# Spreading the inverse RMS norm over the partitions: a row in DRAM, written and read back, in place of two transposes

## The reference

```python
def rms_norm(x, g):
    y = x * rsqrt(mean(x * x, axis=-1) + EPS)
    return y * g

def swiglu(x, w_gate, w_up, w_down):
    return (silu(x @ w_gate) * (x @ w_up)) @ w_down

for l in range(2):
    x = x + 0.5 * swiglu(rms_norm(x, ffn1_norm[l]), ffn1_w_gate[l], ffn1_w_up[l], ffn1_w_down[l])
    ...                                    # the mixing sub-layer
    x = x + 0.5 * swiglu(rms_norm(x, ffn2_norm[l]), ffn2_w_gate[l], ffn2_w_up[l], ffn2_w_down[l])
```

## Time and profile before

| | us |
|---|---|
| median of three executions | 1039.33 |
| the profiled execution | 1040.34 |
| its span, first to last instruction | 1038.5 |
| PE busy | 1032.4 (99%) |
| PEld busy | 891.7 (86%) |
| DVE busy | 718.3 (69%) |
| ACT busy | 586.1 (56%) |
| POOL busy | 61.8 (6%) |
| HBM read | 185.98 MB |

### The profile page before, as it was taken

The page is one execution under the profiler, slowest core; times in us unless marked ns, Lnnn a source line. Parts: engine busy times, 40 slices in busy tenths (PEclk is TensorE's granted clock), DMA queues, the critical chain, the costliest instruction groups (busy, mean ns, idle before and its releaser), DMA issues.

```text
span 1038.5 us, 15559 instructions
## 1 busy us (share of the span) xinstructions
PE 1032.4 (99%) x5648; PEld 891.7 (86%) x5648; DVE 718.3 (69%) x1132; ACT 586.1 (56%) x935; POOL 61.8 (6%) x71
## 2 busy tenths in 40 slices
PE   8999999999999999999999999999999999999998
PEld 7888888998888888888888888889988888888887
DVE  6766666668786876666687666666688868666665
ACT  6555454466963754554565455455678646454552
POOL 0052000121100000000000000001211000000000
PEclk9999999999999999999999999999999999999999
DMA  7665544455435455655445555534454346545541
GB/s 264 248 225 192 204 162 167 140 183 193 146 123 203 173 187 189 205 189 209 179 147 202 202 192 182 210 136 152 154 203 163 122 163 219 205 163 202 191 173 61
DMA packets 35269, 187.53 MB, mean 181 GB/s; under 512 B 4368, under 2 KB 4384, under 8 KB 20128
## 3 DMA queue, kind: packets, MB, share of 16 engines
q1 hardware_dynamic: 34992, 186.51, 51.0%
q0 software_dynamic: 240, 0.53, 0.2%
HBM read 185.98 MB, written 1.05 MB: 180 GB/s over the span
## 4 chain that ended last, share of the span: by engine, by line
PE 99%; DMA 1%; SPq 0%; DVE 0%; ACT 0%; issue 0%
PE ps L1369 96%; PE ps L1803 1%; PE ps L1393 1%; DMA w_raw<-in_w_ffn 1%; PE ps L1832 1%; PE ps L1868 0%; PE ps L1712 0%; PE ps L1704 0%; PE ps L1414 0%; DVE x_cols L999 0%; ACT w_hi L554 0%; SPq L318 0%; SPq L317 0%
## 5 line engine op out<-in xcount | busy, mean ns | idle before, releaser
L1369 PE MATMUL ps<-hT,w_hi 128*128 128x512 f32 x1408 | 341.3, 391 | 1.9 <-ACT w_hi L554 1.9
L1369 PEld LDWEIGHTS ps<-hT,w_hi 128*128 128x128 f32 x1408 | 258.9, 188 | 52.4 <-ACT w_hi L554 2.1
L884 DVE TENSOR_TENSOR w_lo<-w_raw,w_hi 128x2048 fp32r<-128x2048 f32 x82 | 188.0, 2293 | 87.7 <-ACT w_hi L549 87.7
L1369 PEld LDWEIGHTS ps<-hT,w_lo 128*128 128x128 f32 x1408 | 176.8, 188 | 7.5
L1369 PE MATMUL ps<-hT,w_lo 128*128 128x256 f32 x1408 | 178.3, 279 | 0.0
L1369 PE MATMUL ps<-w_hi,hT 128*128 128x512 f32 (+2 forms) x576 | 174.3, 377 | 0.0
L549 ACT ACTIVATE w_hi<-w_raw 128x2048 fp32r<-128x2048 f32 x85 | 162.0, 1906 | 13.9 <-PE ps L1369 13.2
L1369 PE MATMUL ps<-w_lo,aTh 128*128 128x512 f32 x352 | 137.2, 390 | 0.0
L1369 PE MATMUL ps<-w_hi,aTl 128*128 128x512 f32 x352 | 137.0, 389 | 0.0
L1369 PE MATMUL ps<-w_hi,aTh 128*128 128x512 f32 x352 | 136.8, 390 | 0.0
L578 ACT ACTIVATE S<-ps 128x256 f32<-128x256 f32 x88 | 33.7, 383 | 154.6 <-PE ps L1369 154.6
(11 more groups left out here) (168 smaller groups left out, 952.9 us busy)
## 6 DMA issues: line engine op xcount, KB each, us to landing
w_raw<-in_w_ffn SPq DMA_DIRECT2D x85, 1024.0 KB, 4.9
w_raw<-in_w_ffn SPq DMA_DIRECT2D x90, 512.0 KB, 5.7
w_raw<-in_w_gate SPq DMA_DIRECT2D x16, 1024.0 KB, 5.1
w_raw<-in_w_proj SPq DMA_DIRECT2D x16, 592.0 KB, 4.4
w_raw<-in_w_branch SPq DMA_DIRECT2D x8, 1024.0 KB, 4.8
w_raw<-in_w_out SPq DMA_DIRECT2D x8, 1024.0 KB, 4.8
w_raw<-in_w_uq SPq DMA_DIRECT2D x4, 384.0 KB, 3.0
w_raw<-in_w_ffn SPq DMA_DIRECT2D x4, 256.0 KB, 6.6
```

The lines of the kernel that those rows point to most:

```text
L884: dve.tensor_tensor(wl_gu[b], raw_gu[b], wh_gu[b].bitcast(F32), ALU.subtract).then_inc(lo_gu.sem, 1)
L1369: return pe.matmul(dst, w, m, start=start, stop=stop, skip_group_check=True)
```

## The change

In the last three feed-forward sub-layers (layer 0 second half, layer 1 both halves) PE's two transposes and ACT's copy are gone. SP writes `rs` to a DRAM tensor of one row of 256 values (256 elements of 4 bytes, in the order of the tokens, so that the two values of a partition go to places 128 apart), waits until they have landed, and issues a second DMA that reads the row back into all 128 partitions of `rsB`. SP does this between its loads of the gate and up weights of blocks 2 and 3. DVE waits for the second DMA (`rsb_in`), and in these three sub-layers it now adds up both the gate and the up half of block 0 before that wait. The first sub-layer of the kernel keeps its two transposes and the copy (`spread_rs_first`). Nothing else differs.

```diff
--- before.py
+++ after.py
@@ -202,8 +202,10 @@
         gate4_first = signal("gate4_first", 1)
         uq1_first = signal("uq1_first", 1)
         rs_done = signal("rs_done", 3 * RS_STEPS)
-        rsb_ps = signal("rsb_ps", 2)
-        rsb_done = signal("rsb_done", 2)
+        rsb_ps = signal("rsb_ps", 0)
+        rsb_done = signal("rsb_done", 0)
+        rs_written = signal("rs_written", 16 * 2)
+        rsb_in = signal("rsb_in", 16 * 2)
         z_done = signal("z_done", 2 * FB)
         gate_full = signal("gate_full", KC // 2)
         ht_ps = signal("ht_ps", 3 * KC)
@@ -308,6 +310,12 @@
             bank, half = (X_AT_FIRST if layer + n == 0 else X_AT)[c]
             return ps[:, bank, half * SEQ:(half + 1) * SEQ]
 
+        rs_row = nc.dram_tensor("rs_row", (1, SEQ), F32, kind="Internal").ap()
+
+        def spread_count(layer, w):
+
+            return 16 * (2 * layer + w)
+
         block = ctx.enter_context(nc.Block())
 
 
@@ -368,6 +376,14 @@
                         sp.wait_ge(lo_d.sem, lo_d.at(l - 1, 2 * FB - 2 + b))
                     load_d((2 * l + w) * FB + b, b)
 
+            def spread_rs(l, w):
+
+                sp.wait_ge(rs_done.sem, rs_done.at(l, 2 * w * RS_STEPS))
+                with nc.allow_non_contiguous_dma(reason="256 values, once a sub-layer"):
+                    sp.dma_start(rs_row.rearrange("b (t p) -> p (b t)", p=P), rs[:, :]).then_inc(rs_written.sem, 16)
+                sp.wait_ge(rs_written.sem, spread_count(l, w))
+                sp.dma_start(rsB[:, :], rs_row.to_broadcast([P, SEQ])).then_inc(rsb_in.sem, 16)
+
             def load_ffn_rest(l, w):
                 o0 = (0, FFN2_0)[w]
                 first = 0
@@ -383,6 +399,8 @@
                 for b in range(2):
                     sp.wait_ge(lo_gu.sem, lo_gu.at(l, o0 + 2 * first + b))
                     load_gu(row0 + b, b)
+                    if l + w > 0 and b == 0:
+                        spread_rs(l, w)
                 sp.wait_ge(lo_d.sem, lo_d.at(l, w * FB + 2 * first))
                 load_d(row0, 0)
                 with sp.Fori(first + 1, FB // 2 - 1) as i:
@@ -624,9 +642,9 @@
 
                     act.activation(scrap[:, 0:1], scrap[:, 1:2], func)
 
-                def spread_rs(w):
-
-                    act.wait_ge(rsb_ps.sem, rsb_ps.at(l, w))
+                def spread_rs_first():
+
+                    act.wait_ge(rsb_ps.sem, 1)
                     act.activation(rsB[:, :], ps[:, RS_BANK, 0:SEQ], ACT.Copy).then_inc(rsb_done.sem, 1)
 
                 def ffn(w, split_following):
@@ -640,7 +658,7 @@
                         third_high(0)
                         third_high(1)
                         load_table(ACT.Silu)
-                        spread_rs(0)
+                        spread_rs_first()
                         gate_silu(0, 0, 0)
                         split_d(0, 0, 0)
                         prod_high(0, 0, 0)
@@ -665,7 +683,6 @@
                     else:
                         split_d(n, 0, 0)
                         load_table(ACT.Silu)
-                        spread_rs(w)
                         gate_low(n, 0, 0)
                         up_low(n, 0, 0)
                         gate_silu(n, 0, 0)
@@ -1018,7 +1035,7 @@
                         gate_fold(0, 0, 0)
                         up_fold(0, 0, 0)
                         third_low(0)
-                        dve.wait_ge(rsb_done.sem, rsb_done.at(l, 0))
+                        dve.wait_ge(rsb_done.sem, 1)
                         gate_scaled(0, 0, 0)
                         third_low(1)
                         up_times(0, 0, 0)
@@ -1041,9 +1058,11 @@
                         prod_low(0, 0, 3)
                     else:
                         split_d(n, 0, 0)
-                        dve.wait_ge(rsb_done.sem, rsb_done.at(l, w))
-                        gate_z(n, 0, 0)
-                        up_prod(n, 0, 0)
+                        gate_fold(n, 0, 0)
+                        up_fold(n, 0, 0)
+                        dve.wait_ge(rsb_in.sem, spread_count(l, w))
+                        gate_scaled(n, 0, 0)
+                        up_times(n, 0, 0)
                         prod_low(n, 0, 0)
                         gate_z(n, 0, 1)
                         split_gu(n, 0, 2)
@@ -1407,9 +1426,9 @@
                     pe.wait_ge(x_done.sem, x_done.at(layer, 4 * n + (h + 1) * TT - 1 - 2 * TT))
                     transposed(layer, n, h)
 
-                def spread_rs(w):
-
-                    pe.wait_ge(rs_done.sem, rs_done.at(l, 2 * w * RS_STEPS))
+                def spread_rs_first():
+
+                    pe.wait_ge(rs_done.sem, rs_done.at(0, 0))
                     for t in range(TT):
                         ins = pe.transpose(ps[:, RS_BANK, t * P:(t + 1) * P], rs[:, t:t + 1].to_broadcast([P, P]), ident[:, :])
                     ins.then_inc(rsb_ps.sem, 1)
```

## The result

The changed kernel takes 1073.45 us (median of five runs, 1072.39 to 1074.33) against 1039.37 us of the kernel before on the same chip: a ratio of 1.0325, 95% interval 1.0314 to 1.0337. The prediction was 1038.64 us and its range ended at 1040.8. The profiled execution took 1072.5 us, 1.0 us less than its median, and that of before 1.0 us more than its own; so the span grew by a little less than the median, from 1038.5 to 1070.7 us.

The account below looks back on a forecast made before the run. PE was taken to bound the kernel, so 3 x 0.23 = 0.69 us of transposes came off in full, the DMAs (4.4 us) being hidden: median 1039.33 - 0.69 = 1038.64 us, range 1038.2 to 1040.8.

Parts of the forecast that it names:

- What bounds the kernel, and what the transposes cost: PE sets the pace, with two waits at the very start; two transposes cost it 0.23 us in each of three sub-layers.
- the 0.69 worked out: Us taken off PE's list by removing the transposes: 3 x 0.23 in the three changed sub-layers.
- By when rsB is needed: DVE's multiplication by rsB may start at 348.50, 531.80 and 862.50 us without making PE wait at block 0's down product.
- budgets of 5.40, 4.97 and 5.39: Us from the end of POOL's power to the latest harmless multiplication by rsB, in the three changed sub-layers.
- What the two DMAs take: Write 2.1 us, read back 2.2 us, handovers 0.1 us: 4.4 us in all, hidden from PE.
- high end of 6.4 us: Upper bound for the write, from posq_i, a transfer of 256 4-byte values on POOL's queue in the other direction.
- its 5.2 us: Upper bound for the read back, from a smaller broadcast row (rows, 36 KB) among weight loads.
- the 11.7 us of both: Both DMAs at their upper bounds plus handovers, 6.4 + 5.2 + 0.1: 19.3 us late in all, net +18.6 us (1058).
- Rival C: Slow write of single 4-byte values, 6.4 us: rsB late by 10.3 us, net +9.6, about 1049.0 us; chance 0.10.
- What else moves: DVE's multiplication starts 0.6 us later; SP's load for block 3 goes at about 345.6, not 345.41, covered by 1.6 us.
- The range: Execution 1038.2 to 1040.8 us, upwards to 5.95 us from POOL's power to the multiplication, leaving out the slow write, 0.10.

Follow-up runs that it names:

- e4: The changed kernel without its two DMAs and DVE's wait for them, three sub-layers reusing the first one's rsB: 1038.55 us against 1039.39 before.
- probe1: The kernel before plus single DMAs behind its last store, each waited for: 256 x 4 B landed in 8.2 and 8.4 us side by side, 1.5 us 512 B apart.
- probe2: The kernel before plus single DMAs behind its last store, with other pitches and rows: 1 KB written as one run landed in 1.1 us.
- e5: The changed kernel with the 256 values written 64 B apart and the row's first 1024 B read back, so not the norm: 1040.48 us.
- e8: The kernel before, with its transposes, plus the write of rs to DRAM, read by nobody and not waited for until the program's end: 1052.14 us.
- e1: The kernel before, with its transposes, plus the write of rs to DRAM, which SP waits for and nobody reads: 1056.79 us.
- e3: The changed kernel with both DMAs and the wait between them issued from GpSimd's queue in place of SP's: 1081.27 us, one run.
- e2: The changed kernel with each partition's two values written side by side (128 pieces of 8 B) and rsB read at a stride of two: 1050.31 us.
- e9: The changed kernel writing 8 B every 16 B into a 2 KB row, multiplying by every second pair, block 3's load held until rsB landed: 1041.07 us.

## Why the prediction was wrong, point by point

- **What bounds the kernel, and what the transposes cost:** right. PE's eight high matmuls take 1.85 us without them. e4 gained 0.84 us for the 0.69 worked out; its interval reaches none, but its trace shows 0.6 us.
- **By when rsB is needed:** right, and to a few hundredths. With c, as in the prediction, for the way from the end of POOL's power to the multiplication, the changed kernel took c = 357.01 - 341.69 = 15.32 us, then 14.75 and 14.97. Less the budgets of 5.40, 4.97 and 5.39 that is 9.92, 9.78 and 9.58 us late; PE waited 9.89, 9.75 and 9.54.
- **What the two DMAs take:** this is the step that failed. The write was put at 2.1 us, "since it shares queue, direction and an almost quiet DMA", and took 7.9 to 10.2. The read was put at 2.2 and took 5.0 to 6.8. The write lies beyond its high end of 6.4 us each time, the read beyond its 5.2 us in two of three, and c beyond the 11.7 us of both. The output's store was the wrong neighbour: its pieces are whole 2 KB runs, and probe1 shows that the density of short pieces sets the time of a write. `posq_i` has the size of element but not the direction; no run reads 256 single values out of DRAM by themselves, so its 6.4 us say nothing certain of the write. For the read I took the price from transfers whose 128 pieces come from different places; 1 KB from one place takes 2.8 to 3.2 us alone (probe1, probe2), 3.8 with a load behind it (e5), and 5 or more behind the dense write of 4-byte values.
- **Rival C** (chance 0.10) had the right place of the loss, a slow write of single 4-byte values and a late `rsB`, and its sign came true: the first transfer had more than 4 us. Its reason was not the one found. It lets each value be handled by itself, a price by number; probe1 shows that the same 256 values take 1.5 us when they lie 512 B apart. And its size was off: 10.3 us late in all, where 29.2 were measured, because `posq_i` was no better a neighbour and because it left the read at 2.2. It also left out what a stop of PE costs besides its length, 4.6 us at the lower clock and 0.5 us of lost overlap, which no row of before shows, since PE stood there for at most 1.9 us, at the very start.
- **What else moves:** the empty queue ahead of the write was right, but I priced only what stood before it and not what stood behind. The load of block 3 went out at 352.32 and not at about 345.6, and e8 shows that even when it goes out in time it lands in 12.0 us behind the write.
- **The range** let the unknown of this change reach up to c = 5.95 us only, though my own bounds went to 11.7. With the two prices unseen in any row, a chance of 0.10 for all of that was too little.

On the page "DMA: Bandwidth & Descriptors" of the Trainium skill, the section "Rules for kernel authors" says that a strided last dimension becomes one descriptor for each element. The profile agrees: packets under 512 B rose from 4368 to 5232, by 864, which is 3 x 256 for the values and 16 for each of the six new DMAs; e1, with the three writes alone, has 816 more, 3 x 256 and 3 x 16. The section "Specifications" gives 512 B as the least transfer for the full rate and says that below it the engine reads, modifies and writes. No run shows that step itself, and the runs are finer than the limit: 128 pieces of 64 B landed in 1.4 to 2.0 us and 256 of 4 B, 512 B apart, in 1.5 us. Size alone did not make them slow, density did.

## What to carry to other kernels

A small transfer is priced by its pattern at the DRAM side and not by its bytes: before a few values are sent through DRAM, look for a row of the same direction and the same piece size, and if there is none, let the range reach to the far bound or measure the one transfer by itself. Keep short writes apart (here 64 B or more) or join them into longer pieces. A slow write also delays the loads issued behind it (12 us and more in place of 4.9), even where nobody waits for it and even from another queue, and a stop of PE costs more than its length (here 1.7 us more).

## What the runs showed of the hardware that I had not expected

- 256 values of 4 B written side by side into DRAM take 8.1 to 8.6 us, 512 B apart 1.5 us; 128 of them side by side are no faster (7.7 to 7.9 us).
- That write slows a read of the same row after it has landed: 5.0 to 5.2 us, and 2.8 to 3.0 us the second time. Behind a write of the row as one run the read takes 2.9 to 3.1 us.
- While it is in flight, the weight loads issued behind it move 36 GB/s in all (e8), and 39 GB/s when it is on GpSimd's queue and they are on SP's (e3).
- One partition of SBUF to all 128 by DMA takes 6.5 us for 1 KB each, more than the same from DRAM (2.8 to 3.2 us).
- DVE's multiplication of 128x256 float32 values took 425 ns with one operand at a stride of two (e2), as dense, and 616 ns with two of every four (e9).
